# 104 gathered tokens for 96, a second top 16 over 64 pair sums, and one-hots from ScalarE

## What is computed

```python
q = (hc @ wq).reshape(T, 8, 2, 128)
s1 = einsum('thd,hnd->thn', q[:, :, 0], sub_keys[:, 0])     # 128 keys each
s2 = einsum('thd,hnd->thn', q[:, :, 1], sub_keys[:, 1])
v1, i1 = top_k(s1, 16)
v2, i2 = top_k(s2, 16)
cand = (v1[..., :, None] + v2[..., None, :]).reshape(T, 8, 256)
sc, ci = top_k(cand, 16)
e = take(i1, ci // 16) * 128 + take(i2, ci % 16)
g = softmax(sc)
act = gelu(einsum('td,thkd->thk', hc, exp_u[e]))
out = einsum('thk,thkd->td', g * act, exp_v[e])
```

## Time and profile before

| | us |
|---|---|
| median of 3 runs | 829.61 (828.95 to 829.66) |
| the profiled execution | 834.14 |
| its span, first to last instruction | 832.4 |
| PE busy | 794.7 (95%) |
| VectorE busy | 571.9 (69%) |
| ScalarE busy | 169.5 (20%) |
| GpSimd busy | 229.1 (28%) |
| moved by DMA | 294.30 MB, mean 354 GB/s |

### The profile page before, as it was taken

One profiled execution on the slowest core, in us unless ns is written; L12 is line 12 of the kernel. 1 busy time (PEld: TensorE's weight loads), 2 busy tenths in 40 slices (PEclk: granted clock), 3 DMA queues, 4 the chain that ended last, 5 costly groups with the idle time before them and its releaser, 6 DMA issues.

```text
span 832.4 us, 14517 instructions
## 1 busy us (share of the span) xinstructions
PE 794.7 (95%) x5726; PEld 757.3 (91%) x5726; DVE 571.9 (69%) x1146; ACT 169.5 (20%) x444; POOL 229.1 (28%) x224
## 2 busy tenths in 40 slices
PE   6999999899999999689999999999999999999996
PEld 4988779889999999689999999899888889999996
DVE  4958879788994999668889898655444543444413
ACT  4464475552111112012211111000000000000003
POOL 2000000000002445444444435733332223343400
PEclk9999999999999999799999999999999999999998
DMA  8998873559978989999999999999999999999971
GB/s 330 405 381 320 366 328 128 220 211 376 395 261 252 412 308 356 308 371 377 408 408 390 387 381 389 409 409 408 409 409 409 409 409 409 410 408 408 409 307 51
DMA packets 77215, 294.30 MB, mean 354 GB/s; under 512 B 8799, under 2 KB 11103, under 8 KB 75868
## 3 DMA queue, kind: packets, MB, share of 16 engines
q1 hardware_dynamic: 48614, 191.52, 58.9%
q0 software_dynamic: 28000, 101.23, 31.5%
q10 hardware_dynamic: 534, 0.62, 0.2%
HBM read 291.25 MB, written 1.56 MB: 352 GB/s over the span
## 4 chain that ended last, share of the span: by engine, by line
PE 64%; DMA 22%; DVE 10%; issue 2%; ACT 1%; POOL 1%; ACTq 0%; SPq 0%; DVEq 0%
PE banks L1235 22%; PE banks L1264 19%; DMA raw<-in_v_b 16%; DMA rows<-in_u_rows,idx 4%; PE banks L980 3%; PE banks L898 3%; DVE rows L1719 3%; PE banks L1247 2%; PE banks L933 2%; PE banks L976 2%; PE banks L903 1%; PE banks L1049 1%; DVE sc_w L1374 1%; PE banks L874 1%; PE banks L919 1%
## 5 line engine op out<-in xcount | busy, mean ns | idle before, releaser
L1264 PE MATMUL banks<-act,raw 128*128 128x160 f32 x2048 | 294.9, 303 | 6.8 <-issue 1.7
L1264 PEld LDWEIGHTS banks<-act,raw 128*128 128x128 f32 x2048 | 281.7, 191 | 18.8 <-DMA raw<-in_v_b 16.6
L1235 PE MATMUL banks<-hT,raw 128*128 128x160 f32 x2048 | 286.8, 302 | 0.0
L1235 PEld LDWEIGHTS banks<-hT,raw 128*128 128x128 f32 x2048 | 282.6, 192 | 0.0
L1742 DVE SCALAR_TENSOR_TENSOR row_sums<-rows,weight,row_sums 128x1024 f32<-128x1024 f32 x94 | 120.8, 1285 | 138.4 <-DMA rows<-in_v_b,idx 137.2
L568 POOL DMA_INDIRECT rows<-in_u_rows,idx x96 | 121.5, 1266 | 174.3 <-DVE dots L1719 83.2
L568 POOL DMA_INDIRECT rows<-in_v_b,idx x96 | 99.7, 1038 | 168.1 <-PE banks L1264 85.9
L1719 DVE CUSTOM_DVE_ANT_0 rows<-rows,h_rows 128x1024 f32<-128x1024 f32 x96 | 114.9, 1220 | 28.4 <-DMA rows<-in_u_rows,idx 25.4
L830 ACT ACTIVATE turned<-banks,ccol 128x256 f32<-128x256 f32 x8 | 3.8, 471 | 282.6 <-PE banks L1264 282.6
L776 ACT ACTIVATE act<-banks 128x160 f32<-128x160 f32 (+19 forms) x123 | 33.1, 270 | 128.2 <-PE banks L1235 120.7
L549 POOL DMA_DIRECT2D h_lines<-h_stage x1 | 0.5, 519 | 204.9 <-ACT h_stage L801 204.9
(11 more groups left out here) (235 smaller groups left out, 793.1 us busy)
## 6 DMA issues: line engine op xcount, KB each, us to landing
raw<-in_u_t SPq DMA_DIRECT2D x128, 512.0 KB, 9.7
raw<-in_v_b SPq DMA_DIRECT2D x128, 512.0 KB
wq<-in_wq SPq DMA_DIRECT2D x2, 4096.0 KB, 18.3
sh_w<-in_w_mod SPq DMA_DIRECT2D x8, 512.0 KB, 13.2
sc_w<-in_w_mod SPq DMA_DIRECT2D x8, 512.0 KB, 12.6
win<-in_w_in SPq DMA_DIRECT2D x8, 512.0 KB, 14.3
win<-in_w_in SPq DMA_DIRECT2D x1, 4096.0 KB, 20.8
sc_w<-in_w_mod SPq DMA_DIRECT2D x2, 2048.0 KB, 23.1
```

Of the source, the lines that this page charges most:

```text
L1235: last = nc.tensor.matmul(dst, raw[spot_of[n]][:, c * P:(c + 1) * P], hT[:, c, 0:MANY], start=(c == 0), stop=(c == DC - 1))
L1264: return nc.tensor.matmul(chunk_place(c)[:, 0:MANY], raw[spot_of[BLOCKS + j]][:, c * P:(c + 1) * P], act[:, j, :], start=(j == 0 and c < 4 ...
```

## The change

KINDS becomes (64, 32, 8): FEW is 104, MANY 152, and there are 104 gathers from each table, 19 groups of gates, and a third copy of lines (behind u block 67, the kind of 32 still behind 64). `row_sums` of the third kind takes a `raw` spot, so that 8 instead of 9 can be used to the end. Of the 256 sums only 64 are formed, those of row 0 with 16, rows 1 to 3 with 8, rows 4 to 7 with 4 and rows 8 to 15 with 1 column. The row's key is then found by thresholds: the position is compared (is_ge) with each row's first position, and the differences `rise` between neighbouring keys are added up; the column by masking with 15, 7, 3 or 0. Both reductions become four halving additions. ScalarE makes the low part of oh2g, eight copies with a scale for each group. The order of the late products, dot products and one-hots among the blocks is changed, and so are the constants.

```diff
-KINDS = (64, 32)
+KINDS = (64, 32, 8)
-IN_SORT = 26
+IN_SORT = 22
-H2_LATER = (64,)
-EXPERTS_OUT = 22
-EXPERTS_IN = 24
-EXP_AT = 52
-SORT_SKIP = 2
-TURN_AT = 60
-GATE_AT = 65
+H2_LATER = (64, 67)
+EXPERTS_OUT = 17
+EXPERTS_IN = 19
+EXP_AT = 42
+SORT_SKIP = 4
+TURN_AT = 54
+GATE_AT = 60
+PAIR_ROWS = ((0, 1, 16), (1, 4, 8), (4, 8, 4), (8, 16, 1))
+PAIRS_AT = (0, 16, 40, 56)
+PAIRS_KEPT = 64
+PACE_FROM = 46
-PACE = 1.36
-PACE_U = 1.0
-BEFORE_TURN = 3
+PACE = 1.26
+PACE_U = 0.95
+BEFORE_TURN = 6
...
-        AFTER_WQ0 = [(16384 + n * D, GATE_AT) for n in range(4)] + [(22528, ROWS_AT - 1), (23552, STREAM), (8192, 8192 // MANY)]
+        AFTER_WQ0 = [(16384 + n * D, GATE_AT) for n in range(4)] + [(22528, ROWS_AT - 1), (23552, ROWS_AT - 1), (8192, 8192 // MANY)]
...
-                    pool.wait_ge(block_used, TURN_AT + int((i - EARLY - 4) * PACE_U))
+                    pool.wait_ge(block_used, PACE_FROM + int((i - EARLY - 4) * PACE_U))
...
+            def low_onehots(g):
+
+                sc.wait_ge(second_ready, g + 1)
+                if g == 0:
+                    sc.wait_ge(cT_out, TT + 1)
+                else:
+                    sc.wait_ge(gates_ready, g)
+                for k in range(GT):
+                    t = g * GT + k
+                    last = nc.scalar.activation(oh2g[:, 1, k // PT, :, k % PT], oh2[:, k // PT, :, k % PT], ACT.Copy,
+                                                scale=part_low[:, t:t + 1])
+                last.then_inc(low_ready, 1)
+
             for n in range(1, BLOCKS + 1):
                 gelu(n - 1)
+                if group_at(n - 1 - GATE_AT + EVERY) is not None:
+                    low_onehots(group_at(n - 1 - GATE_AT + EVERY))
...
                 pe.wait_ge(onehot_ready, g + 1)
+                pe.wait_ge(low_ready, 16 + g + 1)
...
-                link(nc.vector.tensor_tensor(cand[:, :, :, :], spread(halves_v[:, 0], 3, TOPK),
-                                             spread(halves_v[:, 1], 2, TOPK), ALU.add))
+                for (first, end, wide), start in zip(PAIR_ROWS, PAIRS_AT):
+                    tall = end - first
+                    ins = nc.vector.tensor_tensor(
+                        cand[:, :, start:start + tall * wide].rearrange("p h (a b) -> p h a b", b=wide),
+                        spread(halves_v[:, 0, :, first:end], 3, wide), spread(halves_v[:, 1, :, 0:wide], 2, tall), ALU.add)
+                link(ins)
...
-                    link(nc.vector.tensor_reduce(chosen[:, t, half, :], hit[:, :, :, :], AX.X, ALU.add))
+                    for wide in (8, 4, 2):
+                        link(nc.vector.tensor_tensor(hit[:, :, :, 0:wide], hit[:, :, :, 0:wide], hit[:, :, :, wide:2 * wide],
+                                                     ALU.add))
+                    link(nc.vector.tensor_tensor(chosen[:, t, half, :].rearrange("p (h k) -> p h k", k=TOPK), hit[:, :, :, 0],
+                                                 hit[:, :, :, 1], ALU.add))
...
-                for e in range(GP):
-                    last = nc.vector.tensor_tensor(oh2g[:, e, :, :, :], oh2[:, :, :, :], rows(part_h[:, e, :]), ALU.mult)
-                last.then_inc(onehot_ready, 1)
+                nc.vector.tensor_tensor(oh2g[:, 0, :, :, :], oh2[:, :, :, :], rows(part_h[:, :]), ALU.mult
+                                        ).then_inc(onehot_ready, 1)
...
-            for n in range(GATE_AT + 1, BLOCKS + 2):
+            for n in range(GATE_AT, BLOCKS + 2):
+                g = group_at(n - GATE_AT)
+                if group_at(n - GATE_AT - 2) is not None:
+                    some_dots(2)
+                elif n > GATE_AT + EVERY * NG:
+                    some_dots(2)
                 if GATE_AT < n - 1 < BLOCKS:
                     late(n - 1)
-                g = group_at(n - 1 - GATE_AT)
                 if g is not None:
-                    gate_acts(g)
+                    if g:
+                        some_dots(1)
                     if g + 1 < NG:
                         onehots(g + 1)
-                elif n > GATE_AT + EVERY * NG:
-                    some_dots(2)
-                else:
-                    some_dots(2 if n % (2 * EVERY) == GATE_AT % (2 * EVERY) else 1)
+                if group_at(n - GATE_AT - 1) is not None:
+                    gate_acts(group_at(n - GATE_AT - 1))
```

More of the change, by code:

```diff
@@ L1752, in weights @@
                                         ).then_inc(weight_ready, 1)
-            link(nc.vector.tensor_copy(place_h[:, :], iota[:, 0:TOPK]))
+            nc.vector.tensor_copy(place_h[:, 1, :], iota[:, 0:TOPK])
+            for (first, end, wide), start in zip(PAIR_ROWS, PAIRS_AT):
+                ins = nc.vector.tensor_scalar(place_h[:, 0, first:end], iota[:, first:end], float(wide),
+                                              float(start - first * wide), ALU.mult, ALU.add)
+            link(ins)
             places = [0]
@@ L1772, in _ @@
                 halves_i = top_i[:, :, :].rearrange("p (h two) k -> p two h k", two=2)
-                link(nc.vector.tensor_tensor(cand[:, :, :, :], spread(halves_v[:, 0], 3, TOPK),
-                                             spread(halves_v[:, 1], 2, TOPK), ALU.add))
+                for (first, end, wide), start in zip(PAIR_ROWS, PAIRS_AT):
+                    tall = end - first
+                    ins = nc.vector.tensor_tensor(
+                        cand[:, :, start:start + tall * wide].rearrange("p h (a b) -> p h a b", b=wide),
+                        spread(halves_v[:, 0, :, first:end], 3, wide), spread(halves_v[:, 1, :, 0:wide], 2, tall), ALU.add)
+                link(ins)
                 between()
-                top16(best, best_iu, lambda h: cand[:, h, :, :].rearrange("p a b -> p (a b)"), HEADS, between)
+                top16(best, best_iu, lambda h: cand[:, h, :], HEADS, between)
                 nc.vector.tensor_tensor(gate[:, t, :, :], best[:, :, :],
@@ L1780, in _ @@
                                         ).then_inc(gate_max, 1)
-                nc.vector.tensor_scalar(part_u[:, 0, :, :], best_iu[:, :, :], 4, None, ALU.logical_shift_right)
-                link(nc.vector.tensor_scalar(part_u[:, 1, :, :], best_iu[:, :, :], TOPK - 1, None,
-                                             ALU.bitwise_and))
-                link(nc.vector.tensor_copy(part[:, :, :, :], spread(part_u[:, :, :, :].rearrange("p n h k -> p n (h k)"), 3, 2)))
+                nc.vector.tensor_copy(rise[:, :, 0:1], halves_i[:, 0, :, 0:1])
@@ new lines, in _ @@
+                nc.vector.tensor_tensor(rise[:, :, 1:TOPK], halves_i[:, 0, :, 1:TOPK], halves_i[:, 0, :, 0:TOPK - 1],
+                                        ALU.subtract)
+                nc.vector.tensor_copy(part[:, 0], spread(best_iu[:, :, :].rearrange("p h k -> p (h k)"), 2, 2))
+                nc.vector.tensor_scalar(part_u[:, 0, :, :], best_iu[:, :, :], float(PAIRS_AT[1]), 2.0, ALU.is_lt, ALU.mult)
+                link(nc.vector.tensor_scalar(part_u[:, 1, :, :], best_iu[:, :, :], float(PAIRS_AT[3]), 3.0, ALU.is_lt, ALU.mult))
@@ new lines, in _ @@
+                link(nc.vector.scalar_tensor_tensor(out=part_u[:, 0, :, :], in0=best_iu[:, :, :], scalar=float(PAIRS_AT[2]),
+                                                    in1=part_u[:, 0, :, :], op0=ALU.is_lt, op1=ALU.add))
+                link(nc.vector.scalar_tensor_tensor(out=part_u[:, 0, :, :], in0=part_u[:, 0, :, :], scalar=4.0,
+                                                    in1=part_u[:, 1, :, :], op0=ALU.mult, op1=ALU.add))
+                link(nc.vector.tensor_tensor(part_u[:, 1, :, :], best_iu[:, :, :], part_u[:, 0, :, :], ALU.bitwise_and))
@@ L1785, in _ @@
+                link(nc.vector.tensor_copy(part[:, 1], spread(part_u[:, 1, :, :].rearrange("p h k -> p (h k)"), 2, 2)))
                 for half in range(2):
-                    place = spread(place_h[:, :].rearrange("p (q two) -> p q two", two=2), 1, HK)
+                    place = spread(place_h[:, half, :].rearrange("p (q two) -> p q two", two=2), 1, HK)
                     link(nc.vector.tensor_tensor(hit[:, :, :, :].rearrange("p h k (q two) -> p (h k) q two", two=2),
-                                                 spread(part[:, half], 2, TOPK // 2), place, ALU.is_equal))
+                                                 spread(part[:, half], 2, TOPK // 2), place,
+                                                 ALU.is_equal if half else ALU.is_ge))
@@ L1790, in _ @@
                     between()
                     link(nc.vector.tensor_tensor(hit[:, :, :, :], hit[:, :, :, :],
-                                                 spread(halves_i[:, half], 2, TOPK), ALU.mult))
-                    link(nc.vector.tensor_reduce(chosen[:, t, half, :], hit[:, :, :, :], AX.X, ALU.add))
+                                                 spread(halves_i[:, 1] if half else rise[:, :, :], 2, TOPK), ALU.mult))
+                    for wide in (8, 4, 2):
```

(3 more changed lines are left out.)

14 lines of the change are left out of this document (8 added, 6 removed).

## The result

| | us | ratio to the kernel before, 95% interval |
|---|---|---|
| before, median of 4 | 829.63 (828.95 to 831.68) | |
| changed, median of 4 | 843.72 (843.10 to 844.64) | 1.0158 (1.0140 to 1.0175) |
| changed, profiled execution | 844.01, span 842.2 | |

The changed kernel is 14.1 us slower. I had forecast 830.2 us, with a range up to 838, and the result lies 5.7 us above that range. By the ratio in the table it is 13.1 us on 830, where the quotient of the two medians gives 14.1: single microseconds are not to be read from such figures. In the profiled executions the step is 9.8 us of span (842.2 against 832.4); the execution of before that was profiled lay 4.5 us above its median, that of after lies 0.3 above.

A forecast was written before the change was run, and what follows sets the result against it. The prediction took the stream of transfers, at 409 GB/s full rate, to bound the kernel. Its terms, 21.8 - 17.2 - 4.0 = +0.6 us on 829.6, gave 830.2 us, with a range of 823 to 838.

The forecast's parts named there:

- The bytes, 21.8 us: Transfer stream: 16 more gather units and one copy of lines, 17 x 1.282 us, add 21.8 us.
- The idle time filled, 17.2 us: Transfer stream: unused time falls from 37.2 to 20.0 us, saving 17.2 us.
- 240 to 252: Stretch before the first gather: only 3 blocks can be sent for, leaving 8.2 us of the stream unused.
- the start of the gathers: Stream as gathers begin, first one at 252 us: 3.0 us left unused.
- rival (2): New copy of 8 lines is as slow as the old, some gathers wait: 4.4 to 6 us more, 836; chance 0.17.
- The end, -4.0 us: Kernel's end: last four v blocks begin 1.9 us after the stream's end instead of 5.9, saving 4.0 us.
- The sums of the few, 4.4 us: PE's sums near the kernel's end, after block 119: 4.4 us where they took 3.5.
- The step from the execution to the median, -4.5 us: From profiled execution to median of runs: the median taken as 4.5 us below the execution.
- rival 4: Gates' stage: VectorE or ScalarE falls behind, PE waits for one-hots with blocks landed; 9.5 us, 840; chance 0.05.
- (1): Transfer stream: idle time fills better and last blocks follow at once, 5 to 6 us less, 825; chance 0.15.
- (3): Whole kernel: PE is the bound, its 35 us come through until the stream stops it, 822; chance 0.04.
- (5): Sort: it gets no shorter, small strided operations costing as much; gathers 8 us later, 837; chance 0.04.

The follow-up runs named there:

- experiment 1: Changed kernel without its third kind (kinds 64 and 32, 96 tokens) and PACE 1.36; 821.32 us, ratio 0.9887 to the kernel before.
- experiment 2: Kernel before with only the third kind of 8 tokens and PACE 1.26 added; 851.56 us, ratio 1.0255.
- experiment 4: Changed kernel with the copy of 32 lines written as four loads of 32 partitions; 838.46 us, ratio 1.0096 to the kernel before.
- experiment 10: Experiment 1 (96 tokens) with the copy of 32 lines in four loads; 814.33 us, ratio 0.9782 to the kernel before.
- experiment 6: Changed kernel with PACE 1.15 in place of 1.26, so late gathers leave sooner; 850.38 us, ratio 1.0225 to the kernel before.
- experiment 7: Changed kernel with the sums of the kinds of 64 and 32 moved behind v blocks 95 and 118; 837.60 us, ratio 1.0067 to the kernel before.
- Experiment 5: Changed kernel with the sums of the kind of 64 moved behind v block 95; 839.11 us, ratio 1.0103 to the kernel before.
- experiment 11: Experiment 10 (96 tokens, copy in four) with the sums of the kind of 64 moved behind v block 95; 813.30 us, ratio 0.9780 to the kernel before.
- experiment 3: Experiment 1 (96 tokens, shorter sort) with the order constants of the kernel before; 824.88 us, ratio 0.9917 to the kernel before.
- experiment 9: Experiment 8 with PACE 1.34 in place of 1.30; 839.86 us, ratio 1.0094 to the kernel before.
- experiment 8: Changed kernel (104 tokens) with copy of 32 lines in four, both larger kinds' sums moved and PACE 1.30; 836.90 us, ratio 1.0063 to the kernel before.

## Why the prediction was wrong

The sum was 21.8 - 17.2 - 4.0 = +0.6 us, on a start of 829.6.

- **The bytes, 21.8 us.** Right: by part 3 of the pages the queues carry 303.3 MB instead of 294.3, 9.0 MB more, 22.0 us at 409 GB/s. Experiments 1 and 2 put the whole third kind at 22.4 and 21.2 us on two different kernels. That these are so close to the bytes is partly luck, for each holds idle time that was filled and a later end besides (experiment 1 above).
- **The idle time filled, 17.2 us.** Nearly right: 15.3. 240 to 252 and the start of the gathers went as forecast; the first gather left at 250.59 (252), the gates' values were there at 310.9 (305 to 312), the first gates began at 330.72 (330), no wait at the turn. The missing 1.9 us are a balance: where the slow copies are, from 324 to 356, 7.0 us were lost where I had 4.4; from 520 on 1.4 where I had nothing; and ahead of the copies less than I had taken. In the stretch of the copies experiment 1, with one slow copy, loses 5.3, so that some 1.7 go with the third kind's copy. With the copy of 32 in four the two versions (experiments 4 and 10) lose 4.6 and 2.9, the same 1.7. So a part of rival (2) was true, 1.7 us where I had taken 0 and kept 4.4; that this is the access pattern of the small copy, and not that it is one more load in the same place, is not shown. The rule of the Trainium skill (DMA: Bandwidth & Descriptors, Rules for kernel authors) about the outermost count agrees with the trace for the copy of 32 lines as far as experiment 4 goes: its slowest 8 us move 326 GB/s instead of 251, and not 409. For the new one of 8 lines the forecast read it as nothing lost, against these 1.7.
- **The end, -4.0 us: the step that failed.** It measured +4.2, so 8.2 us of the miss are here, and I had its sign wrong. The step said that "after block 119 it has four blocks and the sums of the few (3.5, now 4.4 us) to do, 12.8 us, while 8 or 9 units of stream remain, 11 us". The last gather is out at 800.78, and block 120 begins at about 807.0, when the stream has 5.6 us left, 4 units and not 8. I had counted in units of stream with gathers among the blocks, at 2.30 us a block, up to the end. But the gathers stop before the blocks do, and after the last one the stream brings a block in 1.28 us, for which PE needs 2.08. Each block behind that point puts PE 0.8 us further behind. So the stream had 5.6 us left and not 11: 5.4 of the 8.2 us. From PE's last wait on it is 6 blocks, 4.8 us of difference in pace. Experiment 6 moves that point by 8 blocks and pays 5.6 us for it.
- **The sums of the few, 4.4 us within that step.** They took 7.2, the other 2.8 of the 8.2 us. The 48 matmuls are 5.4 to 5.6 us at the full clock (experiments 4 and 2: 5.42 and 5.58). The prediction gives no working for its 4.4; by their number, from the 3.49 us of 32 in the earlier trace rows, it would have been 5.2, and a matmul of 8 columns is hardly shorter than one of 32 (16 of each: 1.85 and 1.87 us in experiment 7). Another 1.8 are the lower clock. Experiment 5 takes back both the moved part and the clock.
- **The last pieces** from 822.66 on took 19.5 us, 0.8 less than before. Together, with 1.8 for the later end of the stream, 1.8 + 8.2 - 0.8 = 9.2 us: the whole miss against the execution that I had worked from, 834.7 forecast and 844.0 measured.
- **The step from the execution to the median, -4.5 us.** I had carried over that the profiled execution of before lay 4.5 us above its median. That of after lies 0.3 above, so the other 4.2 us of the 13.5 come from here. Single executions scatter by some us (experiment 4: 834.7 to 840.7; the 13 of the kernel before beside experiment 10, 828.7 to 835.3). The granted clock has a part in it: of those 13 the three at a mean of 0.988 took 832.1 to 835.3 us, the six at 0.991 or 0.992 828.7 to 832.9, and the profiled one of before stands at 0.988. What makes the clock differ was not found out.
- **ScalarE and VectorE** (rival 4): PE's idle time in 386 to 520, ahead of u blocks and ahead of the gates, is shown by two groups of the trace, and one-hots are not in it. The last line is ScalarE's timeline at the end of the u stage:

```profile
L1256 PE MATMUL banks<-hT,raw 128*128 128x152 f32 x793 | 113.5, 299 | 11.2 <-DMA raw<-in_u_t 5.6 <-ACT gelu_out L780 4.7 <-issue 0.9
L1269 PE MATMUL banks<-oh2g,oh 128*128 128x128 f16 x208 | 14.0, 218 | 0.0
...
519.02 0.30 ACT L780 ACTIVATE gelu_out<-banks 128x152 f32<-128x152 f32 x1 [5.74 <-DVE act L1881]
```

Half is the wait for blocks; 4.7 us are two waits for the last gelus before the v stage (1.89 and 2.82 us), with the clock at 0.58 from 513 to 524. ScalarE in turn waited 4.83 and 5.74 us there for VectorE's late products (L1881), and VectorE has two dot products ahead of each, which wait 1.05 to 2.29 us for their gathers. So rival (4) was true in this one place, by the order of VectorE's work and not by its amount. The v stage begins at 523.6 and not near 510. By the rates this costs nothing while the stream is full: it moves 407 GB/s in these 11 us.
- **Rivals (1), (3) and (5)** fell: the idle time filled no better than forecast, PE was not the bound with 104 tokens, and the sort got shorter, by 8.4 us for the first tile where I had 9.6 (its experts are ready at 239.7, before at 248.1). With 96 tokens (3) is half true: PE is busy nearly all the time, and the stream is full as well until shortly before its end (experiments 1, 10 and 11).

## What to carry to other kernels

Where a stream of transfers bounds a stage, price more bytes at their full time first, and then look at where the last of the optional transfers (here the gathers) stands: behind it the stream brings blocks faster than the engine can take them, and every block left there costs the difference between the two paces. The last optional transfer can also come too late: with 104 tokens and the other edits in place, 0.04 more of PACE cost about 3 us. An engine pays for a wait on one slow transfer with the hole and sometimes with a lower clock behind it; how much of that reaches the end depends on whether the stream lets the engine catch up. Here the third kind's bytes and the rest of the change are edits of opposite sign: the rest (the shorter sort, ScalarE's one-hots, the new order) without the third kind, with one load cut in four, is 2.2% faster than the kernel before.

## What the runs showed of the hardware

- One load of 512 KB with a repetition of four outermost holds all transfers down, at a DMA share of 1.02 to 1.03, so the page shows it as full use: 280 GB/s over 15 us in the kernel before, 299 and 301 over 16 us in experiment 1, and 273 and 251 over 16 us in the changed kernel, which has the load of 8 lines beside it. Cut in four, the same bytes left 326 and 333 GB/s (experiment 4), and 344 and 380 without the load of 8 lines (experiment 10).
- TensorE's granted clock can fall with PE busy all the time. In or right behind the sums of the few, f32 matmuls of 64, 32 and 8 columns, it fell to 0.54 for 6 us in the changed kernel, to 0.50 from 826 to 832 in experiment 6 and from 830 to 832 in experiment 2 (48 of them each), and to 0.54 from 812 to 814 in the kernel before (32). It kept 1.00 in the profiles of experiment 4 (48), of 1, 3, 5 and 10 (32), and of 7 and 11 (16). So the number of such matmuls alone does not decide it, and the cause is open.
- Waits of 9.62 us (experiment 9), of 6.22 us (the changed kernel, 0.50 from 350 to 354) and of 5.30 us (experiment 1, 0.50 from 358 to 362) were followed by work at the lower clock. In the profile of experiment 8 a wait of 3.32 us at 352.00 was not (2.33 us for the block, 1.00 from 352 to 356), while the clock fell to 0.69 for 4 us behind one of 2.09 us and the 16 matmuls of the sums after it.
